# Two-layer block with routed experts on one core: rotating queries and keys by VectorE shuffles in two steps of a head, and the order of differences, maxima and ScalarE's work

## The reference

```python
dq = apply_partial_rope(da_q.reshape(B, S, 4, 2, 64), cos, sin)     # and dk likewise
s = einsum('bhmqd,bhmkd->bhmqk', qb, k) * scale                     # 4 heads, 2 maps m each
a = softmax(where(key_chunk <= q_chunk, s, neg), axis=-1)
a = a[:, :, 0] - lam * a[:, :, 1]
y_b = einsum('bhqk,bhkd->bhqd', a, v)
y_b = rmsnorm(y_b, g_subln) * (1.0 - lam_init)

def apply_partial_rope(t, cos, sin):      # 16 of the 64 columns are rotated, half = 8
    r1, r2 = t[..., :half], t[..., half:16]
    rot = concatenate([r1 * cos - r2 * sin, r2 * cos + r1 * sin], axis=-1)
    return concatenate([rot, t[..., 16:]], axis=-1)
```

## Time and profile before

| what | before |
|---|---|
| median of 3 timed runs | 2491.66 us (2491.55 to 2495.01) |
| the profiled execution: its time, its span | 2489.01 us, 2487.2 us |
| TensorE matmul busy, share of the span | 2276.0 us, 92% |
| VectorE, ScalarE, GpSimd busy | 1001.7, 585.3, 408.7 us (40%, 24%, 16%) |
| differential attention, layer 0 and layer 1 | 162.10 to 294.56 us and 935.71 to 1068.10 us |

### The profile page before, as it was taken

One profiled execution on the slowest core, in us unless ns is written; L12 is line 12 of the kernel. 1 busy time (PEld: TensorE's weight loads), 2 busy tenths in 40 slices (PEclk: granted clock), 3 DMA queues, 4 the chain that ended last, 5 costly groups with the idle time before them and its releaser, 6 DMA issues. The chain is left out here.

```text
span 2487.2 us, 29142 instructions
## 1 busy us (share of the span) xinstructions
PE 2276.0 (92%) x11776; PEld 1690.1 (68%) x11776; DVE 1001.7 (40%) x1730; ACT 585.3 (24%) x1211; POOL 408.7 (16%) x404
## 2 busy tenths in 40 slices
PE   7989999589888999999689889899999999999998
PEld 5666788445447767688544446787767887888886
DVE  5545533411135444643511115445653334322234
ACT  2433401211123342420311103423441002100011
POOL 2101121112111101121112212011101221111121
PEclk9999999799999999999889999899999999999999
DMA  4114535699982202233689994332222333233321
GB/s 149 52 52 103 134 105 203 254 416 422 423 321 68 76 26 70 65 94 134 260 345 422 422 394 163 80 86 70 84 69 72 102 100 99 85 102 94 101 94 68
DMA packets 291540, 402.85 MB, mean 162 GB/s; under 512 B 31306, under 2 KB 230730, under 8 KB 273478
## 3 DMA queue, kind: packets, MB, share of 16 engines
q1 hardware_dynamic: 276444, 373.31, 42.2%
q0 software_dynamic: 10176, 16.81, 1.8%
q10 hardware_dynamic: 4778, 10.76, 1.6%
HBM read 388.99 MB, written 30.15 MB: 169 GB/s over the span
## 5 line engine op out<-in xcount | busy, mean ns | idle before, releaser
L146 PE MATMUL banks<-h_split,w_high 128*128 128x512 f32 x2624 | 825.9, 396 | 2.8 <-PEq L3044 1.7
L146 PEld LDWEIGHTS banks<-h_split,w_high 128*128 128x128 f32 x2624 | 480.8, 188 | 104.5 <-issue 8.2
L198 DVE TENSOR_TENSOR w_low<-w_raw,w_high 128x1024 fp32r<-128x1024 f32 (+1 forms) x264 | 317.1, 1203 | 514.9 <-POOL w_high L187 514.8
L187 POOL CAST w_high<-w_raw 128x1024 fp32r<-128x1024 f32 (+1 forms) x264 | 277.0, 1050 | 1449.7 <-PE banks L146 1329.6
L146 PE MATMUL banks<-h_split,w_low 128*128 128x512 f32 x1312 | 512.1, 390 | 0.0
L146 PEld LDWEIGHTS banks<-h_split,w_low 128*128 128x128 f32 x1312 | 246.2, 188 | 52.7
L146 PE MATMUL banks<-w_high,op_split 128*128 128x512 f32 x736 | 228.0, 390 | 1.1 <-DVE mg_part L1278 1.1
L1848 PE MATMUL banks<-expert_ring,ex_xsT 128*64 128x256 f32 x1472 | 174.7, 391 | 23.3 <-DMA expert_ring<-in_w_exp_up 20.2
L146 PEld LDWEIGHTS banks<-w_high,op_split 128*128 128x128 f32 x736 | 138.1, 188 | 31.1 <-DVE mg_part L1278 2.4
L1848 PEld LDWEIGHTS banks<-expert_ring,ex_xsT 128*64 128x64 f32 x1472 | 104.9, 140 | 79.4 <-DMA expert_ring<-in_w_exp_up 22.6
L146 PE MATMUL banks<-w_low,op_split 128*128 128x512 f32 x368 | 143.3, 389 | 0.0
(11 more groups left out here) (424 smaller groups left out, 2757.2 us busy)
## 6 DMA issues: line engine op xcount, KB each, us to landing
w_raw<-in_w_in SPq DMA_DIRECT2D x142, 512.0 KB, 4.0
expert_ring<-in_w_exp_gate SPq DMA_DIRECT2D x46, 1024.0 KB
expert_ring<-in_w_exp_up SPq DMA_DIRECT2D x46, 1024.0 KB
expert_ring<-in_w_exp_down SPq DMA_DIRECT2D x46, 1024.0 KB, 17.6
w_raw<-in_w_gu SPq DMA_DIRECT2D x44, 512.0 KB, 4.0
region<-in_w_exp_gate SPq DMA_DIRECT2D x20, 1024.0 KB
region<-in_w_exp_up SPq DMA_DIRECT2D x20, 1024.0 KB
region<-in_w_exp_down SPq DMA_DIRECT2D x20, 1024.0 KB
```

The lines of the kernel that those rows point to most:

```text
L146: last = nc.tensor.matmul(out, left, right, start=(start and n == 0), stop=(stop and n == 2), skip_group_check=True)
L187: self.nc.gpsimd.tensor_copy(self.high[:, i % self.SPLIT, 0:n], self.raw[:, i % self.RAW, 0:n]).then_inc(self.high_ready, 1)
L198: self.nc.vector.tensor_tensor(self.low[:, i % self.SPLIT, 0:n], self.raw[:, i % self.RAW, 0:n], self.high[:, i % self.SPLIT, 0:n].bitcast ...
```

## The change

The exchange is no longer a matmul. VectorE makes it with `stream_shuffle`, which permutes partitions within each 32 by one list (`ROPE_PAIRS`), from the raw queries or keys into `qT` or `kT`, multiplies there by sin, and adds the cos part. The signs move into the frequencies, and so into the table of sines. The constant matrix, its load (one of seven of its group) and the 16 swaps go. Queries are rotated at t = 1 and keys at t = 2. The difference of step s stands ahead of the maxima of step s + 1. ScalarE keeps its order in odd steps; in even steps it does the scaled result of s - 1, the copy of s, then the exponentials of s + 1.

```diff
+ROPE_PAIRS = [*range(8, 16), *range(8), *range(16, 32)]
...
-        (k.rope_swap[:], t["c_rope_swap"])]))
...
         def project(head, part, bank):
             for n, c in part:
                 if c == 0 and head > 1:
-                    pe.wait_ge(sem["rope_step"], 4 * (head - 1) + 3 + n)
+                    pe.wait_ge(sem["rope_step"], 4 * (head - 1) + 2 + 2 * n)
+                    if n == 0 and head > 2:
+                        pe.wait_ge(sem["y_out"], head - 2)
...
-        swap(0, 0, 0)
-        swap(0, 1, 1)
...
                 if t == 2:
-                    if head:
-                        pe.wait_ge(sem["y_out"], head)
-                    swap(head + 1, 0, 5)
-                    swap(head + 1, 1, 7)
                     fill(1)
...
+        def take_turned(s):
+            n = (s % NT + 1) * P
+            act.wait_ge(sem["turned"], s + 1)
+            nc.scalar.activation(diffT[:, s % 2, 0:n], k.ps[:, 4, 0:n], ACT.Copy).then_inc(sem["diffT_ready"], 1)
...
-            if s + 1 < steps:
+            if s % 2 == 0:
+                if s:
+                    scale_result(s - 1)
+                take_turned(s)
                 exps(s + 1)
-            if s:
+            else:
+                if s + 1 < steps:
+                    exps(s + 1)
                 scale_result(s - 1)
-            act.wait_ge(sem["turned"], s + 1)
...
+                take_turned(s)
...
-        def sin_part(head, n, bank):
+        def sin_part(head, n):
             dst = (qT, kT)[n][:, head % 2, :]
+            nc.vector.stream_shuffle(dst, raw[:, n, :], ROPE_PAIRS).then_inc(sem["swapped"], 1)
             dve.wait_ge(sem["swapped"], 2 * head + n + 1)
-            nc.vector.tensor_tensor(dst, k.ps[:, bank, :], sinT[:], ALU.mult).then_inc(sem["rope_step"], 1)
+            nc.vector.tensor_tensor(dst, dst, sinT[:], ALU.mult).then_inc(sem["rope_step"], 1)
...
         for n in (0, 1):
             cos_part(0, n)
-        for n in (0, 1):
-            sin_part(0, n, n)
+            sin_part(0, n)
...
+            difference(s)
             if s + 1 < steps:
                 maxima(s + 1)
-            difference(s)
             if t == 0 and head:
                 norm(head - 1)
             if t == 1 and head:
                 low_result(head - 1)
             if head + 1 < heads:
-                if t == 2:
-                    cos_part(head + 1, 0)
-                    cos_part(head + 1, 1)
-                    sin_part(head + 1, 0, 5)
-                    sin_part(head + 1, 1, 7)
                 if t in (1, 3):
                     st.split_low(dve, 21 + 3 * head + t // 2)
+                if t in (1, 2):
+                    cos_part(head + 1, t - 1)
+                    sin_part(head + 1, t - 1)
             if t == 0 and head:
                 st.split_low(dve, 20 + 3 * head)
...
-            freq[head + i] = freq[head + half + i] = inv[i]
+            freq[head + i], freq[head + half + i] = -inv[i], inv[i]
```

More of the change, by code:

```diff
@@ L62, in __init__ @@
         self.chunk_bias = sb("chunk_bias", [P, P], BF16)
-        self.rope_swap = sb("rope_swap", [P, P])
         self.shift = sb("shift", [P, 16])
@@ L244, in load_start @@
         (raw[:, 0, :], t["c_neg_tri"]), (raw[:, 1, :], t["c_strict_bias"]), (raw[:, 2, :], t["c_chunk_bias"]),
-        (raw[:, 3, :], t["c_neg_before"]),
-        (k.rope_swap[:], t["c_rope_swap"])]))
+        (raw[:, 3, :], t["c_neg_before"])]))
 class TileRoots:
@@ L774, in _ @@
             start.issue(sp)
-            sp.wait_ge(start.landed[0], 16 * 7)
+            sp.wait_ge(start.landed[0], 16 * 6)
         @block.gpsimd
@@ L781, in _ @@
             nc.gpsimd.tensor_copy(k.neg_ones[:], raw[:, 4, :])
-            pool.wait_ge(start.landed[0], 16 * 7)
+            pool.wait_ge(start.landed[0], 16 * 6)
             nc.gpsimd.tensor_copy(k.ident_b[:], k.ident[:])
@@ L889, in project @@
                 if c == 0 and head > 1:
-                    pe.wait_ge(sem["rope_step"], 4 * (head - 1) + 3 + n)
+                    pe.wait_ge(sem["rope_step"], 4 * (head - 1) + 2 + 2 * n)
+                    if n == 0 and head > 2:
+                        pe.wait_ge(sem["y_out"], head - 2)
                 st.columns(pe, columns_of(head, n), c, bank)
-        def swap(head, n, bank):
-            if head:
-                pe.wait_ge(sem["raw_ready"], 2 * head + n - 1)
-            nc.tensor.matmul(k.ps[:, bank, :], k.rope_swap[:], raw[:, n, :], start=True,
-                             stop=True).then_inc(sem["swapped"], 1)
         def scores(s):
@@ L1031, in scalar @@
             head, t = divmod(s, NT)
-            if s + 1 < steps:
+            if s % 2 == 0:
+                if s:
+                    scale_result(s - 1)
+                take_turned(s)
                 exps(s + 1)
-            if s:
+            else:
+                if s + 1 < steps:
+                    exps(s + 1)
                 scale_result(s - 1)
-            act.wait_ge(sem["turned"], s + 1)
-            nc.scalar.activation(diffT[:, s % 2, 0:(t + 1) * P], k.ps[:, 4, 0:(t + 1) * P],
-                                 ACT.Copy).then_inc(sem["diffT_ready"], 1)
+                take_turned(s)
             if t == 0 and head == 1 and line_store:
@@ L1066, in cos_part @@
                 .then_inc(sem["rope_step"], 1)
-        def sin_part(head, n, bank):
+        def sin_part(head, n):
             dst = (qT, kT)[n][:, head % 2, :]
+            nc.vector.stream_shuffle(dst, raw[:, n, :], ROPE_PAIRS).then_inc(sem["swapped"], 1)
             dve.wait_ge(sem["swapped"], 2 * head + n + 1)
-            nc.vector.tensor_tensor(dst, k.ps[:, bank, :], sinT[:], ALU.mult).then_inc(sem["rope_step"], 1)
-            dve.wait_ge(sem["rope_step"], 4 * head + 3 + n)
+            nc.vector.tensor_tensor(dst, dst, sinT[:], ALU.mult).then_inc(sem["rope_step"], 1)
+            dve.wait_ge(sem["rope_step"], 4 * head + 2 + 2 * n)
             nc.vector.tensor_tensor(dst, dst, turned_part[:, n, :], ALU.add).then_inc(sem["qk_ready"], 1)
@@ L3297, in constants @@
     half = 8
-    swap = np.zeros((P, P), f)
     freq = np.zeros((P, 1), f)
@@ L3302, in constants @@
         for i in range(half):
-            swap[head + half + i, head + i] = -1
-            swap[head + i, head + half + i] = 1
-            freq[head + i] = freq[head + half + i] = inv[i]
+            freq[head + i], freq[head + half + i] = -inv[i], inv[i]
     lam_init = np.array([[0.8 - 0.6 * math.exp(-0.3 * i)] for i in range(DEPTH)], f)
@@ L3345, in constants @@
         "c_chunk_bias": np.where((r[:, None] < 64) & (r[None, :] >= 64), f(MASKED), f(0)),
-        "c_rope_swap": swap,
         "c_rope_freq": freq,
```

## The result

| what | before | after |
|---|---|---|
| median of 20 runs each | 2492.59 us | 2497.64 us |
| ratio after / before, 95% interval | | 1.0022 [1.0015, 1.0028] |
| the profiled execution | 2489.01 us | 2496.02 us |

A forecast was written before the change was run, and what follows sets the result against it. TensorE's matmul time plus small holes was taken to bound the stage. Per layer -1.65 - 2.1 + 1.4 + 0.7 + 0.25, taken as -1.5, -3.0 in all: 2488.7 us; forecast's own range 2485 to 2494.5, whole range 2480 to 2498.

The forecast's parts named there:

- heads 1 and 2: Queries' rotation delays the difference at t = 2; TensorE waits 2.7 us; each head 0.7 us slower, 1.4 per layer.
- rival 2: The shuffle is dear, each rotation longer by 0.7 us: 3.1 us per layer slower, 2497.9 us; chance 0.12.
- What goes: Swaps leave TensorE: 1.77 us for a pair, 4 pairs per layer, 7.1 us per layer, 14.2 in all.
- The shuffle: On VectorE, 128x512 each: 0.69 us, plus 0.04 semaphore and 0.1 list load, 0.82 in a chain.
- Opening: Start of the stage: TensorE starts the values 1.77 us earlier; gain 1.65, nothing to spare.
- Head 0: Queries' rotation fits between the maxima of t = 2 and t = 3; gain 2.1 us from 26.56.
- Rival 1: Rotation hidden in heads 1 and 2 as in head 0: -14.2 us in all, 2477.5 us; chance 0.14.
- Rival 3: Nothing changes: the little left is taken in by the experts' loads, 2491.7 us; chance 0.12.
- GpSimd: Casts meeting VectorE's two-input SBUF work: 0.25 us added per layer, three places, each hit half the time with 0.19.
- The clock: TensorE's granted clock, read as 1.00 of full throughout the profile; no term for it in the sum.
- Head 3: No rotation or swap; waits of 0.85 and 0.25 us come, one of 0.4 goes: 0.7 us slower.
- faster: Outcome beyond 0.2% (5.0 us) of gain: rival 1 and some 0.11 of the forecast, chance 0.25.

The follow-up runs named there:

- cast_later: The changed kernel with GpSimd's casts of weight pieces 25 and 28 held until the difference of t = 2 is done; 2490.36 us, 0.9999 to before.
- q_first: The changed kernel with the queries' rotation at t = 1 put ahead of the low half of the earlier head's result; 2480.85 us, 0.9951 to before.
- keep_busy: The changed kernel with 12 more unread 128x512 matmuls in front of the turn at t = 2 of heads 1 and 2; 2492.18 us, 0.9996 to before.
- cast_late: The changed kernel with GpSimd's casts of weight pieces 25 and 28 held until the queries' rotation ends; 2496.65 us, 1.0014 to before.
- old_act: The changed kernel with ScalarE's old order in all steps; 2504.87 us, 1.0058 to before.
- old_dve: The changed kernel with VectorE's old order, maxima of the next step ahead of the difference; 2499.87 us, 1.0039 to before.
- both_t2: The changed kernel with both rotations at t = 2, behind the difference and the maxima; 2500.67 us, 1.0032 to before.

## Why the prediction was wrong

The step that failed is the sum of what heads 1 and 2 cost: 0.7 us each by the forecast, 2.6 to 2.8 measured. The wait's mechanism was right; two terms on top of it were missing or far too small. The time, 2497.64 us, lies beyond the forecast's own range (2494.5), and on the side of a loss. That it is within 0.3 us of rival 2's 2497.9, and so inside the whole range, is luck: rival 2's mechanism, a dear shuffle, is not there.

- **What goes: right.** No L896 rows are left. Their 1.77 us show where nothing is paid back: the opening of layer 0 is 1.68 us shorter, head 0 2.36 and 2.29 (2.1 forecast). The 8.9 us less of busy time have matmuls at the lower clock in them.
- **The shuffle: right.** 0.71 us, list load 0.01, the next start 0.75 us after the first; 0.82 had been taken. The shuffles of the stages are 708 to 739 ns. Rival 2, the dear shuffle, is refuted.
- **Opening: right in layer 0** (24.19 us, 24.2 forecast); layer 1 takes 24.78, since a wait of 0.59 for the keys comes in. That is a cast once more. VectorE's and GpSimd's timelines of after there:

```profile
940.56 1.42 DVE L1069 TENSOR_TENSOR da_qT<-da_qT,sin_t 128x512 f32<-128x512 f32 x1
...
940.40 1.04 POOL L187 CAST w_high<-w_raw 128x1024 fp32r<-128x1024 f32 x1 [22.63 <-issue]
```

  The multiply starts 0.16 us behind the cast and takes 1.42 us instead of 0.69, in an opening with nothing to spare. In layer 0 the cast (162.88) was nearly done when the multiply (163.66) started: 0.80.
- **Head 0: right**, 24.20 (24.5 forecast), in both layers.
- **Heads 1 and 2: the wait was right in kind and place**, low half to 0.04 us. In cast_later, with no cast met and the clock held, head 2 took 28.36 and 28.40 us against 28.5. Rival 1, the hidden rotation, is refuted by the waits, and q_first shows what it asked for: the rotation in front of the blocked instruction. Rival 3, that nothing reaches the end, is refuted too: 4.8 us in the stages, 5.05 at the end.
- **GpSimd: mis-sized.** The sum took 0.19 us at half chance for each of three places in a layer. Measured: 0.85 us in each of two places in a layer, 3.4 us in all, and 0.6 in layer 1's opening, where the term had 0.5 for both layers. The row behind the 0.19 was a partial overlap: the sum had begun 0.7 us after the cast's start. The Trainium skill (SBUF — State Buffer, Who interferes with whom) says that such a pair exclude each other until the first is done. That is what the runs show, to within some 0.2 us, in both directions: cast 1.92 instead of 1.04 us, cos part 1.53 instead of 0.69, and a 128x1 instruction 1.00 instead of 0.22. The prediction had named this case and kept it out of the sum.
- **The clock: no term at all.** The prediction took the clock as 1.00 throughout and let TensorE wait for nothing more than the wait. The wait was followed by 3.7 us at 0.55 to 0.60, and costs 1.3 us more each, 5.3 for four places (keep_busy).
- **Head 3: right.** 24.72 and 24.69 us (24.7 forecast, on equal ends), with the copy's wait 0.8 (0.85 forecast).
- **A slip in the chances.** A tenth of the forecast's 0.62 is 0.06, not the 0.11 that was added to rival 1 for "faster". No time hangs on it.

The account closes. Forecast -3.0; four casts +3.4 in place of the 0.5 in the sum, +2.9; four clock losses +5.3; the opening of layer 1 +0.6; head 0 better than forecast, -0.5 in two layers; heads 1 and 2 better by some 0.15 each apart from cast and clock (cast_later's head 2), -0.6. Together +4.7, against 4.8 in the stage's windows and 5.05 by the medians.

What stays open: why a wait of 2.5 us is followed by the lower clock in one head and not in the next.

## What to carry to other kernels

Before work moves up in an in-order list, look at what blocks the list there: put it in front of the instruction that waits, not behind it, and the same instructions cost 17 us less here. A forecast of a wait is not done with its length: count too the clock behind it, and every GpSimd cast that can fall into the chain that ends it, at the cast's full length.

## Hardware behaviour that was not expected

- One wait was enough to bring down the clock of a matmul stream that had run at 1.00. In the stages of after, cast_late, old_act and old_dve it fell to 0.50 behind all 15 waits of 3.2 to 3.6 us, either before the wait's end or some time behind it; in cast_later, both_t2 and old_dve behind 5 of 9 waits of 2.4 to 2.7 us; behind none of the shorter ones, 2.19 us (both_t2, twice) the longest. Twelve matmuls whose result nobody reads, in the wait of 3.3 us, kept it at 1.00 and made the kernel faster: the ratio to before is 0.9996 in place of 1.0022.
- A GpSimd cast that finds VectorE in an instruction with two SBUF inputs waits for its end, and then goes ahead of VectorE's next one, although that one could have followed at once: the stream of VectorE is cut, and pays the cast's length in the middle of a chain.
- The size of the VectorE instruction doesn't matter to this: 128x1 (1.00 us) was blocked like 128x512 (1.53 us). A reciprocal on 128x1, with one input, was not: 0.16 us at 226.46 in q_first, just ahead of the blocked 0.80, while that cast was on.
